# Fourteen products of the identity by itself between two stages of TensorE's work

## The reference, cut to what matters

```python
mod = jax.nn.silu(c) @ w_ada + b_ada                 # c: 1 prompt row and 8 sample rows, w_ada (1024, 3072)
shift, scale, gate = jnp.split(mod, 3, axis=-1)
h = rms_norm(x, norm_g) * (1.0 + scale[:, None]) + shift[:, None]
u = h @ w_in                                         # w_in (1024, 3360)
...
```

## Time and profile before

| | |
|---|---|
| median of three runs | 908.7 us (908.7, 912.08, 903.17) |
| the profiled execution | 903.27 us |
| its span | 901.5 us |
| granted TensorE clock, mean | 0.983 |
| PE busy | 827.9 us (92% of the span), 8505 matmul records |
| DVE, ACT, POOL busy | 528.7, 359.8, 292.9 us |
| DMA | 89.06 MB, 99 GB/s over the span; 301 GB/s in the first 20 us and 343 in the next 20 |

### The profile page before, as it was taken

The page is one execution under the profiler, slowest core; times in us unless marked ns, Lnnn a source line. Parts: engine busy times, 40 slices in busy tenths (PEclk is TensorE's granted clock), DMA queues, the critical chain, the costliest instruction groups (busy, mean ns, idle before and its releaser), DMA issues. The chain is left out here.

```text
span 901.5 us, 20076 instructions
## 1 busy us (share of the span) xinstructions
PE 827.9 (92%) x8505; PEld 542.4 (60%) x8505; DVE 528.7 (59%) x1081; ACT 359.8 (40%) x735; POOL 292.9 (32%) x228
## 2 busy tenths in 40 slices
PE   3999999999989999998999997779999999799787
PEld 2447998877778656657455545544556564554643
DVE  2146652375787744457435446797877868576501
ACT  4041002011211345546223436865666566455413
POOL 2048879355254043326211000147111131203021
PEclk9899999999999999999999999999999999999999
DMA  9952255545020000302952353710020010102102
GB/s 307 344 167 101 77 210 212 198 152 186 1 72 1 24 6 1 94 1 85 327 186 70 102 168 123 205 37 1 15 71 26 14 62 13 62 2 71 61 3 94
DMA packets 45411, 89.06 MB, mean 99 GB/s; under 512 B 4388, under 2 KB 26076, under 8 KB 43210
## 3 DMA queue, kind: packets, MB, share of 16 engines
q1 hardware_dynamic: 38202, 54.94, 18.7%
q0 software_dynamic: 6080, 31.79, 10.1%
q10 hardware_dynamic: 1040, 1.05, 0.4%
HBM read 75.49 MB, written 16.40 MB: 102 GB/s over the span
## 5 line engine op out<-in xcount | busy, mean ns | idle before, releaser
L2147 PE MATMUL PS<-W,hT 128*128 128x512 f32 x256 | 113.0, 594 | 0.3 <-DVE W L1766 0.3
L1108 POOL TENSOR_TENSOR Q<-Q,U 128x512 f32<-128x512 f32 x16 | 20.3, 1270 | 265.0 <-DVE U L1967 265.0
L1933 DVE CUSTOM_DVE_ANT_0 PS<-PS,consts 128x640 f32<-128x640 f32 (+5 forms) x96 | 77.3, 836 | 32.2 <-PE PS L2552 31.8
L2147 PEld LDWEIGHTS PS<-W,hT 128*128 128x128 f32 x256 | 47.9, 190 | 56.0 <-issue 54.8
L1419 ACT ACTIVATE hT<-PS,small 128x128 f32<-128x128 f32 (+7 forms) x64 | 46.9, 742 | 48.8 <-DVE small L1933 46.5
L2519 PE MATMUL PS<-U,Y 128*128 128x512 f32 x128 | 61.9, 617 | 0.8 <-ACT OTb L1426 0.8
L2519 PE MATMUL PS<-U,Q 128*128 128x512 f32 x128 | 58.8, 598 | 0.0
L1419 ACT ACTIVATE T<-PS,small 128x640 f32<-128x640 f32 (+4 forms) x64 | 41.7, 661 | 32.4 <-DVE small L1933 32.1
L1616 DVE SCALAR_TENSOR_TENSOR U<-T,small,U 128x512 f32<-128x512 f32 x48 | 46.0, 958 | 1.7
L1949 DVE STREAM_TRANSPOSE hT<-hT 128x1024 f32<-128x1024 f32 (+6 forms) x29 | 42.4, 1482 | 2.0 <-ACT hT L1419 1.8
L2519 PEld LDWEIGHTS PS<-U,Q 128*128 128x128 f32 x128 | 23.6, 190 | 30.4 <-issue 30.4
(11 more groups left out here) (535 smaller groups left out, 1901.6 us busy)
## 6 DMA issues: line engine op xcount, KB each, us to landing
W<-in_w_in SPq DMA_DIRECT2D x4, 2048.0 KB, 7.9
W<-in_w_ada SPq DMA_DIRECT2D x7, 1024.0 KB, 13.0
U<-in_x_prompt SPq DMA_DIRECT2D x8, 512.0 KB, 11.2
W<-in_w_ada SPq DMA_DIRECT2D x2, 2048.0 KB, 8.5
U<-in_state_win_kv POOLq DMA_DIRECT2D x8, 512.0 KB, 5.2
W<-in_x_prompt SPq DMA_DIRECT2D x8, 512.0 KB, 3.3
out_y_prompt<-W SPq DMA_DIRECT2D x8, 512.0 KB, 3.0
out_new_win_sample<-in_state_win_kv POOLq DMA_DIRECT2D x1, 4032.0 KB, 24.3
```

What stands on the lines that cost most here:

```text
L1108: nc.gpsimd.tensor_tensor(Q3[:, i, :], Q3[:, i, :], spare, ALU.add).then_inc(s_added, 1)
L1933: ins = nc.vector.tensor_tensor_reduce(x, x, strip(u), 1.0, -NEG, ALU.add, ALU.min, sneg_m[u % 2][:, m:m + 1])
L2147: ins = nc.tensor.matmul(bank(z_bank(u)), hT3[:, k, i * P:(i + 1) * P], w, start=(k == 0), stop=(k == KT8 - 1))
```

## The change: what it does, and the diff

After `mod(0)` and before the loop over `p`, TensorE gets fourteen matmuls with the identity as stationary and as moving operand, 128x128 by 128x128 in 4-byte floats, into the first 128 columns of PSUM bank 0. They wait for no semaphore and raise none, and nothing reads their result. Bank 0 is next written by the first product L2042, with `start=True`. No other engine's list changes.

```diff
             mod(0)
+            for _ in range(14):
+                nc.tensor.matmul(bank(0, 0, P), ident, ident, start=True, stop=True)
             for p in range(4):
                 if p == 0:
                     for h in range(2):
                         pe.wait_ge(s_xn, 2 * h + 2)
```

## The result

The median went from 905.15 to 910.19 us over 22 runs each: a ratio of 1.0066, with a 95% interval of 1.0044 to 1.0088. The change makes the kernel slower by 0.7%, where a gain of 0.4% was forecast. The profiled execution of the changed kernel took 913.79 us, 3.6 us above its own median. So the two profiles differ by 10.5 us where the medians differ by 5.0, and about half of what they show side by side belongs to these two executions and not to the change.

A forecast was written before the change was run, and what follows sets the result against it. TensorE, busy 92% of the span, was taken to bound the kernel; 0.49 + 3.04 - 0.15 - 0.03 = 3.35 us gained, so the median goes from 908.7 to 905.4 us, range 898.5 to 911.5.

The forecast's parts named there:

- the part on the added products: After `mod(0)`: 28 records cost 3.25 us at full clock, 6.0 at half, covered by TensorE's wait until 17.75.
- From there ... all moves together: After transposes L2006: TensorE's stage releases DVE, POOL's L889 and the transfers, so the 3.35 us gain carries through.
- the sum: Whole kernel: 0.49 + 3.04 - 0.15 - 0.03 = 3.35 us gained.
- the rival that I gave 0.12: Clock falls back to half before L2042, leaving only 0.49 us from the second transposes: 908.2 us, chance 0.12.
- The term of eight products: First L2042 products: eight records at full clock take 3.48 us in place of 6.52, starting `mod(1)` at 25.47.
- The cost of the products: Added products from 14.43: 3.25 us at full clock or 6.0 at half, ending at 17.7 or 20.4; 3.25 taken.
- DVE and POOL: Around POOL's sums L899: L1479 passes at 53.14, later scalings wait for 57.90, L2006 starts at 60.8, 3.35 us gained.
- the boundary I had named for 2.2 us: End of a POOL sum at 55.5: if DVE's L1479 gets through only there, the gain is 2.2 us.
- The rival that ended slower: Added products run at half clock, end at 20.4 and delay L2042 by 2.8 us: 911.5 us, chance 0.09.
- the stall: TensorE's wait near 267 us, with or without a clock drop: up to 1.7 us either way, nothing added.

The follow-up runs named there:

- N = 78: The kernel before with 78 1x1 products (312 instructions) at the head of TensorE's list; ratio 1.0066 against the kernel before.
- the change with 18: The changed kernel with 18 1x1 products at the head of TensorE's list, 128 added instructions together; ratio 0.9960 against the kernel before, median 899.05 us.
- nine in before: The kernel before with nine identity products ahead of the last transposes of the first stage; ratio 1.0102 against the kernel before.
- The change and nine: The changed kernel with nine more identity products ahead of the last transposes of the first stage; ratio 1.0098 against the kernel before.
- N = 24: The kernel before with 24 1x1 products (96 instructions) at the head of TensorE's list; ratio 1.0036 against the kernel before.
- N = 32: The kernel before with 32 1x1 products (128 instructions) at the head of TensorE's list; ratio 1.0006 against the kernel before.
- tiny products: The change's fourteen calls at the same place, but 9x9 by 9x9 instead of 128x128; ratio 1.0074 against the kernel before.
- seven products: The change with seven identity products in place of fourteen; ratio 1.0046 against the kernel before.

## Why the prediction was wrong

**The step that failed** is in the part on the added products: "No semaphore is touched, so nothing queues behind them but TensorE's own list", and with it "From there ... all moves together". The 28 records were priced by their time in the place where they stand, and as instructions at nothing. They are 56 instructions, and they move every later instruction of TensorE by 56 places in the blocks in which its stream arrives. The small value products of attention are 8448 instructions, 33 blocks, and TensorE gets through a run of 128 records in 2.1 us. Whether a block's end falls into such a run or into a wait decides on a stall, of 1.1 us on average. The price was no term of the sum and in no rival. In the two profiles it is 6.3 us: 91.1 us within these products in place of 84.8. The change as a whole lost 0.66%, 6 us, with its early gain in it, and the runs with the same 56 or 312 instructions without the change's work give 0.66 to 1.01%.

**The gain was mis-sized, by the rival that I gave 0.12.** The clock was up at 18 us but fell back as the first product (L2042) began, at 21.9, where I had it stay up. The term of eight products, put at 3.04 us saved, gave 1.2 (5.30 us in place of 6.52); `mod(1)` started at 27.19, not 25.47. And the profile of before was no fair base: of all fourteen it had the latest rise of the clock. Over the profiles, the first L2102 starts at 70.83, 69.30, 69.94, 68.97, 69.11, 69.63 and 68.31 us in the kernels whose first stage is that of before (and its list of work), 69.44 on average, and at 68.88, 68.57 and 68.43 in the three that have the fourteen products and nothing later in the stage, 68.63. So the change is worth about 0.8 us there, not 3.35 (the seven scatter by 2.5 us, so this is rough). One trace couldn't show that; its 10.3 us at half clock should have been an upper end.

**The cost of the products** was nearly right: they end at 17.7, with slack behind, and took 3.80 us, between the two ends. The first five are 0.21 us apart or more, as priced for half clock, the rest 0.11, as priced for full.

**DVE and POOL** went as described, one sum later: L1479 came at 54.26 and left at 55.8, where POOL's third sum ends. That is the boundary I had named for 2.2 us, and the products L2042 did start 2.13 us earlier for it. L1487 was then held in the same way to 58.2, so the scalings came 0.64 us earlier only, the last of their tiles that L2006 needs was done at 62.1, and L2006 started then, 2.0 us earlier.

**The rival that ended slower** had the right sign by luck, by another mechanism: behind the products the clock was full, and nothing was late at 24 us. And my own range, 898.5 to 911.5, does hold the measured 910.19, but only through the scatter that I allowed for: none of its cases had this cause.

**The clock later on** explains a part and not the main one. I had read its fall at the wait as 267.7 us, but the average of 0.65 in that slice gives 267.3; I left the stall without a price and allowed 1.7 us either way. Between the two profiles the clock did cost 4.1 us, at this wait and at 315 us. Over the many runs it costs less: the mean granted clock was 0.979 in the 22 runs of the change and 0.982 in 93 runs of the kernel before, and among runs of one kernel 0.001 less goes with 0.50 us more, so it stands for about 1.8 of the 6.8 us between the mean spans; that is an estimate from the spans and clocks of all runs. In single profiles, the kernel with N = 78 had the clock of before with a long span, and the change with 18 had a low one with a short span:

```profile
core 0: 910.6 us, clock 0.983
```

```profile
core 0: 897.1 us, clock 0.977
```

**What stays open.** Why the 36 instructions of "nine in before" cost as much as 56 is explained only in part: 2 us are their own work, about 3.5 the products (86.7 against 83.2), about 3 the clock, each an estimate, and no run shows why the clock was lower there. The change and nine costs more than N = 24 at nearly the same place (92 and 96) with 2 us of work of its own and 3.4 us more within the products. Nor is it shown what decides in which profiles the clock falls at 315 us. No run changed how the blocks are fetched; that the stops are waits for a block rests on their place, on the packets ahead of them and on the period of 256. The 0.4% of the best kernel is more than the 0.1% that the first stage explains; the rest may be the place in the block, though N = 32 alone shows none of it.

## What to carry to other kernels

An instruction has a price beside its time: in a kernel whose engine streams thousands of small instructions, a hidden instruction added at the front moves the block boundaries for all that follow. Here that was worth from nothing to 1%. Before a small edit is judged by its total time, compare it with a kernel that has as many dummy instructions in a hidden place, and one with a whole block of them. And a gain that rests on where the clock fell and rose in one trace should be bounded by several traces.

## What the runs showed of the hardware that was not expected

- TensorE stops in the middle of a run of products with no wait on a semaphore, after the same record for the same number of added instructions modulo 256: 1.12 and 0.85 us after record 44 with 56, none with 0 or 256. Of 234 such stops in fourteen profiles 219 end at the same place modulo 256 of TensorE's records, 1.0 to 2.8 us after a packet of 16 KB of instructions.
- The granted clock's strip reads 1.00 before its first change, whatever the pace: in the kernel with tiny products, L2000 took 1.72 us at 18.5, against 1.06 in the changed kernel, and both under a strip of 1.00.
- Filling a wait of 3.25 us with products kept the clock full over it (seven products, with 1.23 us of the wait left, did so too), but not over the two gaps of 0.89 and 1.07 us that came 2 us later with little work between. The times of the clock's changes, counted from the start, differ from execution to execution: it rose at 28.4 us in the profile of before and at 25.3 in the changed kernel's.
